# Gate steps of a tile pair spread between the weight units of the next pair, and a fourth quarter-product pair in the first layer

## The chip, the cores and the metric

One NeuronCore of one Trainium2 chip runs the whole program. The metric is the device time of one execution in microseconds, from the runs' own timer. The profiled execution also has a span, from its first instruction to its last.

## The reference, cut to what matters

Four transformer-like layers on one sequence of 512 tokens of 1024 channels, in float32. The first two layers (one with a causal convolution mixer, one with attention) each end in a feed-forward block, and this block is what the change touches:

```python
def conv_gated_ffn(x, w_up, w_gate, conv_w, conv_b, w_down):
    u = x @ w_up                                        # 1024 -> 2816
    g = causal_dwconv(x @ w_gate, conv_w, conv_b)       # three taps per channel
    return (jax.nn.silu(g) * u) @ w_down                # 2816 -> 1024
```

2816 channels are 22 tiles of 128. The last two layers (a gated linear attention beside a latent attention) and the convolution mixer are not touched.

## The kernel before, in words

**Split numbers.** Every weight is fetched as float32 and split into a high part (rounded to fp32r, tile wh) and a low remainder (wl); activations are split in the same way (XH and XL, HH and HL). A 128x128 block of weights then takes three matmuls: high by high, high by the activations' low part, low by high (function block, L618 records them). Activations lie transposed: channels on partitions, the 512 tokens along the free axis.

**The weight stream.** Weights come in units of 8 blocks (NU), in an order written out by hand (weight_order, and ffn_order at L45 for the feed-forward). SyncE fetches unit u to one of 3 raw buffers (L546, raw), once VectorE has made the remainder of unit u - 3. ScalarE rounds it to one of 4 slots (round_to, L1445), which waits until TensorE has used the unit that held the slot before. VectorE makes the remainder (rest_to, L2165). Both engines do this where their own program says so: feed_group(matrix, ks, cols) stands for the blocks that TensorE is then working on, and where one of these blocks is the first of a unit, the engine prepares the unit three further on (AHEAD). All engines run their programs strictly in order, so a step that waits holds up everything written after it.

**Tiles and pairs.** For the tiles f of the feed-forward TensorE makes up(f) and gate(f) over all 512 tokens: 8 blocks x 3 matmuls of 512 columns for each. The first PAIRS[layer] pairs of tiles (f = 2p and 2p + 1; 3 pairs in layer 0, 7 in layer 1, L23) are made by quarter products instead: tokens, input channels and tiles are halved, and seven products of 4 blocks x 3 matmuls of 256 columns replace eight. For a pair and each of the two matrices these are, in TensorE's order:

- A (up) and D (gate), first_products: 8 blocks, 24 matmuls
- C (up) and F (gate), summed_products: 16 blocks of summed weights (matrices tu and tg), 48 matmuls
- E (up of tile 2p + 1) and B (gate of tile 2p + 1, which comes in the next pair), last_product: 4 blocks, 12 matmuls

The order in time is A(p), B(p-1), C(p), D(p), E(p), F(p): 168 matmuls, 56 blocks, 7 units. The results are put together outside TensorE: ScalarE evacuates a bank twice for each matrix (first_out, second_out), VectorE adds five times (first_combined, three_combined, last_combined). The up results stand in sqr[0] and sqr[1], the gate results in gb[0] and gb[1] (acc_s and acc_q). E(p) waits for the second of the sums of three_combined(0, p), C(p)'s last product for first_combined(0, p), B(p-1) for the second sum of three_combined(1, p-1).

**The gate steps.** For each tile (gated, L1547 on ScalarE and L2340 on VectorE): ScalarE's bias step, VectorE's two taps, ScalarE's silu, VectorE's product with up, ScalarE's high part of the product (HH), VectorE's low part (HL). In a pair both engines write these as one piece for each tile: gated(f-2) stands between A(p)'s and C(p)'s units, gated(f-1) right behind B(p-1)'s, each engine waiting for the other at every step, and only then comes the preparation of the units for C(p) and, on ScalarE, the evacuation second_out(0, p).

**The summed weights.** They are made in device memory by GpSimd's DMAs (weight_sums, L3166) in four parts (SUMMED, L25: layer, first and last column group, the unit count at which the part begins, and the count between its steps). Each part is a chain of eight DMAs, alternately a copy and an adding DMA; each waits for the one before it to land. A fetch of a tu or tg piece waits on SyncE until its part is complete (raw, s.tw). Pairs 0 and 1 of layer 0 are part 0, pair 2 is part 1; parts 2 and 3 are layer 1's. A step of part 0 moves 1024 KB, one of part 1 512 KB.

## Time and profile before

| what | value |
|---|---|
| median of 3 runs | 1791.28 us (1789.99 to 1794.4) |
| profiled execution, its own time | 1790.65 us |
| its span | 1788.9 us |
| mean granted clock of TensorE | 0.987 of 2.4 GHz |
| TensorE matmuls, busy | 1742.5 us, 97% |
| VectorE, busy | 1150.7 us |
| ScalarE, busy | 896.7 us |

The profiled execution's time is its span and 1.75 us around it. Busy shares are means over stages with different limits; the stretches of the two feed-forward stages with quarter products are 251 to 330 us and 955 to 1130 us. In the rows a matmul whose moving operand is 256 columns wide is "128x256", and matmuls overlap, so the distance between starts tells the rate, not the duration.

### The profile page before, as it was taken

How to read it: one execution, taken by the hardware profiler on the slowest of the kernel's cores; microseconds unless marked ns; L12 is line 12 of the kernel's file. 1: busy time of each engine (PE TensorE's matmuls, PEld its weight loads, DVE VectorE, ACT ScalarE, POOL GpSimd, SP SyncE). 2: the span in 40 equal slices, each digit the busy share in tenths (PEclk: the TensorE clock that was granted, in tenths of full speed). 3: DMA queues.
4: the chain of work that ended last, by engine and by line, in shares of the span. 5: the costliest groups of instructions: out<-in, count | busy, mean ns of one | idle time of the engine just before them, and what ended most of it. 6: DMA issues, size and time to landing. Idle time of an engine off the chain costs nothing.

```text
span 1788.9 us, 24379 instructions
## 1 busy us (share of the span) xinstructions
PE 1742.5 (97%) x9933; PEld 1449.4 (81%) x9933; DVE 1150.7 (64%) x1812; ACT 896.7 (50%) x1408; POOL 40.2 (2%) x53
## 2 busy tenths in 40 slices
PE   9999998999999999999999888999999999999999
PEld 7877998888888887777788887888898876778766
DVE  6778886644433565887786666643368867657674
ACT  6889755433332355666564444432246454533542
POOL 0000100000000000000200000000000000000000
PEclk9999999999999999999999988999999999999999
DMA  5374265755446643311234353223322222132211
GB/s 212 129 219 112 82 198 155 246 166 165 130 151 190 189 130 118 95 48 60 71 115 145 118 162 128 99 95 107 103 85 92 94 60 71 63 102 85 69 60 47
DMA packets 59663, 213.22 MB, mean 119 GB/s; under 512 B 7072, under 2 KB 7328, under 8 KB 56608
## 3 DMA queue, kind: packets, MB, share of 16 engines
q1 hardware_dynamic: 56096, 169.73, 28.5%
q0 software_dynamic: 3456, 41.95, 8.9%
q8 instruction: 78, 1.28, 0.3%
q14 instruction: 33, 0.27, 0.0%
HBM read 207.45 MB, written 44.04 MB: 141 GB/s over the span
## 4 chain that ended last, share of the span: by engine, by line
PE 79%; DVE 11%; ACT 7%; issue 2%; DMA 1%; SPq 0%; ACTq 0%; DVEq 0%
PE bank L618 79%; DVE wl L2161 3%; ACT tmp L1437 2%; DVE tmp L2152 2%; ACT wh L1437 2%; DVE tmp L2149 1%; DMA wraw<-in_wstream 1%; DVE HL L2161 1%; DVE sqr L2152 1%; ACT taps L1437 1%; DVE XL L2161 1%; PE bank L1382 0%; DMA wraw<-tw 0%; ACT HH L1437 0%; DVE sbl L2161 0%
## 5 line engine op out<-in xcount | busy, mean ns | idle before, releaser
L2161 DVE TENSOR_TENSOR wl<-wraw,wh 128x1024 fp32r<-128x1024 f32 (+1 forms) x294 | 355.3, 1219 | 274.2 <-ACT wh L1437 273.5
L618 PE MATMUL bank<-XH,wh 128*128 128x512 f32 (+1 forms) x1424 | 526.9, 370 | 3.0 <-DVE wl L2161 1.0
L618 PE MATMUL bank<-XL,wh 128*128 128x512 f32 (+1 forms) x1424 | 517.0, 363 | 0.0
L618 PE MATMUL bank<-XH,wl 128*128 128x512 f32 (+1 forms) x1424 | 516.9, 363 | 0.0
L1437 ACT ACTIVATE wh<-wraw 128x1024 fp32r<-128x1024 f32 (+1 forms) x294 | 306.5, 1052 | 318.4 <-PE bank L618 265.8
L618 PEld LDWEIGHTS bank<-XH,wh 128*128 128x128 f32 x1424 | 268.7, 189 | 55.9 <-issue 9.4
L618 PEld LDWEIGHTS bank<-XH,wl 128*128 128x128 f32 x1424 | 268.7, 189 | 42.8
L618 PEld LDWEIGHTS bank<-XL,wh 128*128 128x128 f32 x1424 | 269.0, 189 | 39.8 <-issue 0.7
L618 PE MATMUL bank<-HL,wh 128*128 128x256 f32 (+1 forms) x740 | 223.4, 345 | 34.9 <-DVE sqr L2152 34.9
L618 PE MATMUL bank<-HH,wh 128*128 128x256 f32 (+1 forms) x740 | 223.2, 344 | 0.0
L618 PE MATMUL bank<-HH,wl 128*128 128x512 f32 (+1 forms) x580 | 202.9, 350 | 0.0
L618 PEld LDWEIGHTS bank<-HL,wh 128*128 128x128 f32 x740 | 137.1, 203 | 50.4 <-DVE sqr L2152 36.5
L618 PEld LDWEIGHTS bank<-HH,wh 128*128 128x128 f32 x740 | 135.6, 201 | 14.3 <-DVE Y L2152 0.6
L618 PEld LDWEIGHTS bank<-HH,wl 128*128 128x128 f32 x580 | 113.7, 196 | 13.1
L1437 ACT ACTIVATE tmp<-tmp 128x512 f32<-128x512 f32 (+2 forms) x131 | 72.4, 596 | 91.3 <-DVE tmp L2149 90.9
L2149 DVE SCALAR_TENSOR_TENSOR tmp<-bank,prm,tmp 128x511 f32<-128x511 f32 (+1 forms) x48 | 35.9, 749 | 80.1 <-ACT tmp L1437 79.2
L1437 ACT ACTIVATE tmp<-bank 128x512 f32<-128x512 f32 (+4 forms) x129 | 70.5, 567 | 14.7 <-PE bank L618 12.4
L1437 ACT ACTIVATE tmp<-bank,prm 128x512 f32<-128x512 f32 (+1 forms) x44 | 30.5, 696 | 92.3 <-PE bank L618 92.2
L2152 DVE TENSOR_TENSOR X<-X,bank 128x512 f32<-128x512 f32 (+1 forms) x58 | 38.5, 665 | 39.7 <-PE bank L618 39.7
L618 PE MATMUL bank<-XH,HL 128*128 128x256 f32 x256 | 57.4, 287 | 0.3 <-DVE XL L2161 0.2
L618 PE MATMUL bank<-wh,XH 128*128 128x512 f32 x128 | 50.7, 396 | 0.1
L2161 DVE TENSOR_TENSOR HL<-tmp,HH 128x512 fp32r<-128x512 f32 x44 | 30.5, 692 | 30.7 <-ACT HH L1437 30.7
(375 smaller groups left out, 2438.3 us busy)
## 6 DMA issues: line engine op xcount, KB each, us to landing
wraw<-in_wstream SPq DMA_DIRECT2D x256, 512.0 KB, 3.6
wraw<-tw SPq DMA_DIRECT2D x80, 256.0 KB, 3.2
tw<-in_w POOLq DMA_DIRECT2D x6, 1536.0 KB, 12.6
tw<-in_w POOLq DMA_DIRECT2D x4, 2048.0 KB, 15.5
wraw<-in_wstream SPq DMA_DIRECT2D x22, 256.0 KB, 2.9
tw<-in_w POOLq DMA_DIRECT2D x4, 1024.0 KB, 10.6
tw<-in_w POOLq DMA_DIRECT2D x6, 512.0 KB, 7.9
tw<-tw POOLq DMA_DIRECT2D x2, 1536.0 KB, 7.3
```

Source lines behind the costliest of these rows:

```text
L618: return pe.e.matmul(o, l, r, start=start, stop=stop, skip_group_check=True)
L1437: return act.e.activation(o, i, f, **kw)
L2149: return dve.e.scalar_tensor_tensor(out=o, in0=i0, scalar=sc, in1=i1, op0=op0, op1=op1)
L2152: return dve.e.tensor_tensor(o, i0, i1, op)
L2161: return dve.e.tensor_tensor(o, x, h.bitcast(F32), ALU.subtract)
```

## The change

- PAIRS goes from (3, 7) to (4, 7): tiles 6 and 7 of layer 0 are made by quarter products. Part 1 of the summed weights therefore covers column groups 4 to 8 instead of 4 to 6, at the same starting count and with the same eight steps, each now 1024 KB.
- The first pair of each layer has four empty blocks in place of B, so that in layer 0 each pair begins with a unit. The stream grows from 307 to 311 units; from layer 0's down projection to the end of layer 1 blocks lie half a unit further on than before.
- gated is cut into bias, silu and high on ScalarE and taps, product and low on VectorE, for each tile. The six steps of each of the two tiles of pair p - 1 are placed one by one between the preparations of pair p's units.
- VectorE's three_combined(1, p-1) and ScalarE's second_out(1, p-1) are written at the head of the next pair instead of at the end of their own. The numbering of the sums (SUMS) follows.
- The up results rotate over three buffers (sqr[0], sqr[1] and the new third), since the products of pair p - 1 are now made after part of pair p has been evacuated; first_out and second_out of up wait for the product that last read their buffer.
- TensorE's, SyncE's and GpSimd's programs are unchanged.

```diff
-PAIRS = (3, 7)
-
-SUMMED = [(0, 0, 4, 16, 1), (0, 4, 6, 38, 1), (1, 0, 6, 60, 4), (1, 6, 14, 100, 5)]
+PAIRS = (4, 7)
+
+SUMMED = [(0, 0, 4, 16, 1), (0, 4, 8, 38, 1), (1, 0, 6, 60, 4), (1, 6, 14, 100, 5)]
...
         out += [(up, k, f) for k in range(KD)]
-        if p:
-            out += [(gate, k, f - 1) for k in range(4, KD)]
+        out += [(gate, k, f - 1) for k in range(4, KD)] if p else [None] * 4
         out += [(tu, k, p) for k in range(16)] + [(gate, k, f) for k in range(KD)]
         out += [(up, k, f + 1) for k in range(4, KD)] + [(tg, k, p) for k in range(16)]
...
-    return [(p, 0, 1)] + [(p - 1, 1, 5)] * (p > 0) + [(p, 0, 2), (p, 0, 3), (p, 0, 4), (p, 1, 1), (p, 0, 5), (p, 1, 2), (p, 1, 3), (p, 1, 4)]
-
-
-SUMS = [[x for p in range(n) for x in sums_of_pair(p)] + [(n - 1, 1, 5)] for n in PAIRS]
+    before = [(p - 1, 1, j) for j in (2, 3, 4)] if p else []
+    return before + [(p, 0, 1)] + [(p - 1, 1, 5)] * (p > 0) + [(p, 0, 2), (p, 0, 3), (p, 0, 4), (p, 1, 1), (p, 0, 5)]
+
+
+SUMS = [[x for p in range(n) for x in sums_of_pair(p)] + [(n - 1, 1, j) for j in range(2, 6)] for n in PAIRS]
...
+    m.PP, m.HH, m.HL, m.pts, m.SF, m.third = [], [], [], [], [], []
...
+            m.third.append(sb(ph, f"third{layer}", [128, S]))
...
     m.gb = [m.acc_s, m.acc_q]
+    m.ub = [[[(m.sqr + [t])[(2 * p + j) % 3] for j in range(2)] for p in range(FT // 2)] for t in m.third]
...
-        def gated(f, g):
-
-            n = FT * layer + f
-            u, v = tmp[2 * f % 4], tmp[(2 * f + 1) % 4]
+        def bias(f, g):
+
             act.wait_ge(s.pg_x, 8 * layer + 8)
             if f >= 2:
-                act.wait_ge(s.f_h, n - 1)
-            fn(u[:, :], g[:, :], ACT.Identity, scale=P(f"fcw{layer}", 3 * f + 2), bias=P(f"fcb{layer}", f)).then_inc(s.f_u, 1)
-            act.wait_ge(s.f_conv, n + 1)
+                act.wait_ge(s.f_h, FT * layer + f - 1)
+            fn(tmp[2 * f % 4][:, :], g[:, :], ACT.Identity, scale=P(f"fcw{layer}", 3 * f + 2), bias=P(f"fcb{layer}", f)).then_inc(s.f_u, 1)
+
+        def silu(f):
+
+            u = tmp[2 * f % 4]
+            act.wait_ge(s.f_conv, FT * layer + f + 1)
             fn(u[:, :], u[:, :], ACT.Silu).then_inc(s.f_silu, 1)
-            act.wait_ge(s.f_h, n + 1)
-            fn(HH[:, f, :], v[:, :], ACT.Copy).then_inc(s.f_hi, 1)
-
-        def pair_gated(p, odd):
+
+        def high(f):
+
+            act.wait_ge(s.f_h, FT * layer + f + 1)
+            fn(HH[:, f, :], tmp[(2 * f + 1) % 4][:, :], ACT.Copy).then_inc(s.f_hi, 1)
+
+        def pair_bias(p, odd):
             act.wait_ge(s.u_c, combined(layer, p, 1, 4 + odd))
-            gated(2 * p + odd, m.gb[odd])
+            bias(2 * p + odd, m.gb[odd])
...
         def first_out(g, mat, p):
+            if g == 0 and p >= 2:
+                act.wait_ge(s.f_h, FT * layer + 2 * p - 2)
             act.wait_ge(s.stream, w.done(mat, KD - 1, 2 * p))
-            fn((sqr, m.gb)[g][0][:, 0:256], bank[3 * g][:, 0:256], ACT.Copy).then_inc(s.u_e, 1)
+            fn((m.ub[layer][p], m.gb)[g][0][:, 0:256], bank[3 * g][:, 0:256], ACT.Copy).then_inc(s.u_e, 1)
 
         def second_out(g, mat, p):
+            if g == 0 and p:
+                act.wait_ge(s.f_h, FT * layer + 2 * p - 1)
             act.wait_ge(s.stream, w.done(mat, 15, p))
-            fn((sqr, m.gb)[g][1][:, 0:256], bank[3 * g][:, 0:256], ACT.Copy).then_inc(s.u_e, 1)
+            fn((m.ub[layer][p], m.gb)[g][1][:, 0:256], bank[3 * g][:, 0:256], ACT.Copy).then_inc(s.u_e, 1)
 
         for p in range(PAIRS[layer]):
             f = 2 * p
+            if p:
+                second_out(1, tg, p - 1)
             feed_group(up, range(KD), [f])
             if p:
-                pair_gated(p - 1, 0)
+                pair_bias(p - 1, 0)
             first_out(0, up, p)
             if p:
                 feed_group(gate, range(4, KD), [f - 1])
-                pair_gated(p - 1, 1)
-            feed_group(tu, range(16), [p])
+            feed_group(tu, range(4), [p])
+            if p:
+                pair_bias(p - 1, 1)
+            feed_group(tu, range(4, 12), [p])
+            if p:
+                silu(f - 2)
+            feed_group(tu, range(12, 16), [p])
+            feed_group(gate, range(4), [f])
+            if p:
+                silu(f - 1)
             second_out(0, tu, p)
-            feed_group(gate, range(KD), [f])
+            feed_group(gate, range(4, KD), [f])
+            feed_group(up, range(4, KD), [f + 1])
+            if p:
+                high(f - 2)
             first_out(1, gate, p)
-            feed_group(up, range(4, KD), [f + 1])
-            feed_group(tg, range(16), [p])
-            second_out(1, tg, p)
+            feed_group(tg, range(8), [p])
+            if p:
+                high(f - 1)
+            feed_group(tg, range(8, 16), [p])
+        last = PAIRS[layer] - 1
+        second_out(1, tg, last)
         for f in range(2 * PAIRS[layer], FT):
             feed_group(up, range(KD), [f])
             if f == 2 * PAIRS[layer]:
-                pair_gated(PAIRS[layer] - 1, 0)
+                pair_bias(last, 0)
                 feed_group(gate, range(4, KD), [f - 1])
-                pair_gated(PAIRS[layer] - 1, 1)
+                pair_bias(last, 1)
+                silu(f - 2)
+                silu(f - 1)
+                high(f - 2)
+                high(f - 1)
             feed_group(gate, range(KD), [f])
             act.wait_ge(s.stream, w.done(gate, KD - 1, f))
-            gated(f, bank[gate_bank(f)])
+            bias(f, bank[gate_bank(f)])
+            silu(f)
+            high(f)
...
-        def gated(f, bu, bg):
-
-            n = FT * layer + f
-            u, v = tmp[2 * f % 4], tmp[(2 * f + 1) % 4]
-            dve.wait_ge(s.f_u, n + 1)
+        def taps(f, bg):
+
+            u = tmp[2 * f % 4]
+            dve.wait_ge(s.f_u, FT * layer + f + 1)
             t = dve.mark(stt(u[:, 1:S], bg[:, 0:S - 1], P(f"fcw{layer}", 3 * f + 1), u[:, 1:S], ALU.mult, ALU.add))
             dve.wait_ge(dve.own, t)
             stt(u[:, 2:S], bg[:, 0:S - 2], P(f"fcw{layer}", 3 * f), u[:, 2:S], ALU.mult, ALU.add).then_inc(s.f_conv, 1)
-            dve.wait_ge(s.f_silu, n + 1)
-            tt(v[:, :], u[:, :], bu[:, :], ALU.mult).then_inc(s.f_h, 1)
-            dve.wait_ge(s.f_hi, n + 1)
-            less(HL[:, f, :], v[:, :], HH[:, f, :]).then_inc(s.f_lo, 1)
+
+        def product(f, bu):
+
+            dve.wait_ge(s.f_silu, FT * layer + f + 1)
+            tt(tmp[(2 * f + 1) % 4][:, :], tmp[2 * f % 4][:, :], bu[:, :], ALU.mult).then_inc(s.f_h, 1)
+
+        def low(f):
+
+            dve.wait_ge(s.f_hi, FT * layer + f + 1)
+            less(HL[:, f, :], tmp[(2 * f + 1) % 4][:, :], HH[:, f, :]).then_inc(s.f_lo, 1)
...
-            b, (o, _) = bank[3 * g:3 * g + 3], (sqr, m.gb)[g]
...
+            b, (o, q) = bank[3 * g:3 * g + 3], (m.ub[layer][p], m.gb)[g]
...
-            q = (sqr, m.gb)[g][1]
...
         for p in range(PAIRS[layer]):
             f = 2 * p
+            if p:
+                three_combined(1, p - 1)
             feed_group(up, range(KD), [f])
-            if p:
-                gated(f - 2, sqr[0], m.gb[0])
             first_combined(0, p)
             if p:
+                taps(f - 2, m.gb[0])
+                last_combined(1, p - 1)
+                dve.wait_ge(s.u_c, combined(layer, p - 1, 1, 5))
                 feed_group(gate, range(4, KD), [f - 1])
-                last_combined(1, p - 1)
-                gated(f - 1, sqr[1], m.gb[1])
-            feed_group(tu, range(16), [p])
+            feed_group(tu, range(12), [p])
+            if p:
+                product(f - 2, m.ub[layer][p - 1][0])
+                taps(f - 1, m.gb[1])
             three_combined(0, p)
-            feed_group(gate, range(KD), [f])
+            feed_group(tu, range(12, 16), [p])
+            feed_group(gate, range(4), [f])
+            if p:
+                product(f - 1, m.ub[layer][p - 1][1])
+            feed_group(gate, range(4, KD), [f])
+            feed_group(up, range(4, KD), [f + 1])
             first_combined(1, p)
-            feed_group(up, range(4, KD), [f + 1])
+            if p:
+                low(f - 2)
             last_combined(0, p)
             dve.wait_ge(s.u_c, combined(layer, p, 0, 5))
-            feed_group(tg, range(16), [p])
-            three_combined(1, p)
+            feed_group(tg, range(8), [p])
+            if p:
+                low(f - 1)
+            feed_group(tg, range(8, 16), [p])
+        last = PAIRS[layer] - 1
+        three_combined(1, last)
         for f in range(2 * PAIRS[layer], FT):
             feed_group(up, range(KD), [f])
             if f == 2 * PAIRS[layer]:
-                gated(f - 2, sqr[0], m.gb[0])
+                taps(f - 2, m.gb[0])
+                last_combined(1, last)
+                dve.wait_ge(s.u_c, combined(layer, last, 1, 5))
                 feed_group(gate, range(4, KD), [f - 1])
-                last_combined(1, PAIRS[layer] - 1)
-                gated(f - 1, sqr[1], m.gb[1])
+                taps(f - 1, m.gb[1])
+                product(f - 2, m.ub[layer][last][0])
+                product(f - 1, m.ub[layer][last][1])
+                low(f - 2)
+                low(f - 1)
             feed_group(gate, range(KD), [f])
-            gated(f, bank[(2 + 2 * f) % 6], bank[gate_bank(f)])
+            taps(f, bank[gate_bank(f)])
+            product(f, bank[(2 + 2 * f) % 6])
+            low(f)
```

## Rows read from the trace of the kernel before

**Rows 1.** The page: busy shares, and the chain that ended last by engine
```profile
PE 1742.5 (97%) x9933; PEld 1449.4 (81%) x9933; DVE 1150.7 (64%) x1812; ACT 896.7 (50%) x1408; POOL 40.2 (2%) x53
PE 79%; DVE 11%; ACT 7%; issue 2%; DMA 1%; SPq 0%; ACTq 0%; DVEq 0%
```

**Rows 2.** Waits of TensorE, first layer (244:315), then second (959:1130): total, times, longest
```profile
PE bank L618 <- DVE sqr L2152: 8.7, 2, 4.4
...
PE bank L618 <- DVE sqr L2152: 26.1, 6, 4.4
```

**Rows 3.** Table by stretch: us, busy PE, PEld, DVE, ACT, POOL, clock, DMA, GB/s
```profile
984.95:1012.30 27.35, 23.00 (x170) 22.75 (x169) 17.57 (x26) 12.32 (x17) 0.00 (x0) 0.88 0.41 132
988.00:998.00 10.00, 10.00 (x84) 9.92 (x83) 6.63 (x10) 3.69 (x7) 0.00 (x0) 1.00 0.23 87
1002.50:1008.00 5.50, 5.48 (x25) 5.48 (x26) 3.32 (x5) 1.06 (x1) 0.00 (x0) 0.50 0.87 266
1123.30:1323.00 199.70, 199.70 (x921) 167.03 (x920) 85.89 (x99) 62.98 (x75) 0.00 (x0) 1.00 0.29 98
...
270.16:296.89 26.73, 22.32 (x170) 21.71 (x169) 18.54 (x27) 14.59 (x19) 0.78 (x1) 0.94 0.62 179
296.89:323.24 26.35, 21.98 (x171) 21.74 (x170) 16.99 (x25) 11.73 (x17) 0.53 (x1) 0.94 0.53 193
```

**Rows 4.** TensorE in order of time: start, us, what, [idle before and its releaser]
```profile
1002.52 0.79 PE L618 MATMUL bank<-HL,wh 128*128 128x256 f32 x2 [4.35 <-DVE sqr L2152]
```

**Rows 5.** ScalarE in order of time: round, evacuation, bias step, silu, table load
```profile
983.77 1.06 ACT L1437 ACTIVATE wh<-wraw 128x1024 fp32r<-128x1024 f32 x1 [2.00 <-PE bank L618]
985.15 0.38 ACT L1437 ACTIVATE acc_q<-bank 128x256 f32<-128x256 f32 x1 [0.32 <-PE bank L618]
987.62 0.80 ACT L1437 ACTIVATE tmp<-acc_s,prm 128x512 f32<-128x512 f32 x1
996.32 0.63 ACT L1437 ACTIVATE tmp<-tmp 128x512 f32<-128x512 f32 x1 [1.60 <-DVE tmp L2149]
...
961.03 1.28 ACT L1437 ACT_TABLE_LOAD   x1
```

**Rows 6.** VectorE in order of time: two taps, product, two remainders, two of three sums
```profile
994.75 1.54 DVE L2149 SCALAR_TENSOR_TENSOR tmp<-acc_q,prm,tmp 128x511 f32<-128x511 f32 x2 [0.89 <-ACT tmp L1437]
996.98 0.69 DVE L2152 TENSOR_TENSOR tmp<-tmp,sqr 128x512 f32<-128x512 f32 x1 [0.70 <-ACT tmp L1437]
999.32 2.36 DVE L2161 TENSOR_TENSOR wl<-wraw,wh 128x1024 fp32r<-128x1024 f32 x2 [0.26 <-ACT wh L1437]
1001.60 0.41 DVE L2152 TENSOR_TENSOR sqr<-sqr,bank 128x256 f32<-128x256 f32 x1
1002.04 0.42 DVE L2152 TENSOR_TENSOR sqr<-bank,sqr 128x256 f32<-128x256 f32 x1
```

**Rows 7.** TensorE and the table by stretch, where a shorter gap stood (convolution stage)
```profile
131.44 0.50 PE L618 MATMUL bank<-cinh,HH 32*128 32x512 f32 x4 [0.99 <-DVE cinl L2161]
...
131.00:140.00 9.00, 8.09 (x96) 6.29 (x96) 8.34 (x13) 8.71 (x15) 0.00 (x0) 1.00 0.78 162
```

**Rows 8.** GpSimd's DMAs: three steps of part 0, then part 1's first
```profile
93.71 0.83 POOL L3164 DMA_DIRECT2D tw<-in_w  x1 [13.37 <-DVE wl L2161]
105.95 0.52 POOL L3160 DMA_DIRECT2D tw<-tw  x1 [11.41 <-DMA tw<-in_w]
111.90 0.82 POOL L3164 DMA_DIRECT2D tw<-in_w  x1 [5.43 <-DMA tw<-tw]
...
225.65 0.54 POOL L3160 DMA_DIRECT2D tw<-in_w  x1 [20.12 <-DVE wl L2161]
```

**Rows 9.** DMA issues (size, median us to landing), and ScalarE awaiting a unit beside one
```profile
wraw<-in_wstream SPq DMA_DIRECT2D x256, 512.0 KB, 3.6
tw<-in_w POOLq DMA_DIRECT2D x4, 1024.0 KB, 10.6
...
321.36 1.06 ACT L1437 ACTIVATE wh<-wraw 128x1024 fp32r<-128x1024 f32 x1 [4.40 <-DMA wraw<-in_wstream]
```

More of the change, by code:

```diff
@@ L430, in place @@
         m.cinl = ring(ph, "cinl", 2, [128, PAD + S], FR)
-    m.PP, m.HH, m.HL, m.pts, m.SF = [], [], [], [], []
+    m.PP, m.HH, m.HL, m.pts, m.SF, m.third = [], [], [], [], [], []
     for layer in range(2):
@@ L2347, in gated @@
             stt(u[:, 2:S], bg[:, 0:S - 2], P(f"fcw{layer}", 3 * f), u[:, 2:S], ALU.mult, ALU.add).then_inc(s.f_conv, 1)
-            dve.wait_ge(s.f_silu, n + 1)
-            tt(v[:, :], u[:, :], bu[:, :], ALU.mult).then_inc(s.f_h, 1)
-            dve.wait_ge(s.f_hi, n + 1)
-            less(HL[:, f, :], v[:, :], HH[:, f, :]).then_inc(s.f_lo, 1)
+        def product(f, bu):
[4 more added lines that the diff above has]
+            less(HL[:, f, :], tmp[(2 * f + 1) % 4][:, :], HH[:, f, :]).then_inc(s.f_lo, 1)
         def first_combined(g, p):
-            b, (o, _) = bank[3 * g:3 * g + 3], (sqr, m.gb)[g]
+            b, (o, _) = bank[3 * g:3 * g + 3], (m.ub[layer][p], m.gb)[g]
             dve.wait_ge(s.u_e, 4 * (pairs_before(layer) + p) + 2 * g + 1)
@@ L2359, in three_combined @@
         def three_combined(g, p):
-            b, (o, q) = bank[3 * g:3 * g + 3], (sqr, m.gb)[g]
+            b, (o, q) = bank[3 * g:3 * g + 3], (m.ub[layer][p], m.gb)[g]
             dve.wait_ge(s.u_e, 4 * (pairs_before(layer) + p) + 2 * g + 2)
@@ L2367, in last_combined @@
         def last_combined(g, p):
-            q = (sqr, m.gb)[g][1]
+            q = (m.ub[layer][p], m.gb)[g][1]
             dve.wait_ge(s.stream, w.done(("up", "gate")[g] + str(layer), KD - 1, 2 * p + 1))
```

## The prediction

> **What bounds the kernel now.** The page comes first: TensorE is busy for 97% of the span and carries 79% of the chain that ended last; VectorE and ScalarE carry 18% between them [rows 1]. So the time can fall only where that chain leaves TensorE. The waits say where: TensorE waits for VectorE's sums into sqr six times in the second feed-forward and twice in the first, some 4.4 us each, once in every pair but the first [rows 2]. The table by stretch gives the price. From A(p) to A(p+1) of the second layer, 984.95 to 1012.30, it is 27.35 us [rows 3]. The pair's matmuls are 168, and 84 of their kind take 10.00 us (0.12 us each), so 20.16 us would do: 7.19 us are lost. About 4.5 us are the wait [rows 4]; behind it the clock stands at 0.50 for 5.5 us, the lower level of 1.2 GHz, and 25 matmuls take what 46 would [rows 3]; that is the rest. In layer 0 the two pairs take 26.73 and 26.35 us, an excess of 6.57 and 6.19. The wait is E(p)'s for three_combined(0, p), which both engines reach only after the whole ping-pong of gated(f-1) and two remainders; the rows of VectorE show just this order [rows 6].
>
> A plain tile pair for comparison: 96 matmuls of 512 columns at 199.70 us for 921, 0.217 us each, 20.8 us [rows 3].
>
> **The change, layer 1.** No matmul is added or removed, and each pair's work on VectorE (17.57 us) and ScalarE (12.32 us) stays [rows 3]; it fits under 20.16 us if the order does. I walk one pair, t = 0 at A(p); segments end at A 2.88, B 4.32, C 10.08, D 12.96, E 14.40, F 20.16. Blocks lie so that a unit begins at the fifth block of A, at C's first and ninth, D's first, E's first, F's fifth and thirteenth. Durations are round 1.06, evacuation 0.38, bias 0.80, silu and high 0.63, two taps 1.54, product and low 0.69, remainder 1.2, the second sum ending 0.86 after the first begins [rows 5, 6]; ScalarE starts 0.20 after TensorE has passed a boundary (985.15 against 984.95).
> - ScalarE: second_out(1) from 0.2, round from 1.7 (its slot is free at 1.44), bias(f-2) to 3.5, first_out(0) to 3.7, round from 4.5 to 5.6. VectorE: three sums to 2.2, remainder to 4.0, first_combined, taps(f-2) to 5.8, last_combined to 6.2, remainder to 7.3; ScalarE's bias(f-1) 6.2 to 7.0.
> - The next round may start only when TensorE has passed C's eighth block, 7.20: 7.4 to 8.5. Behind it silu(f-2) to 9.0 and VectorE's remainder to 9.7, product(f-2) to 10.3, taps(f-1) to 11.8. ScalarE's next round waits for C's end and runs 10.3 to 11.4; silu(f-1) 11.9 to 12.5; second_out(0) to 12.8; VectorE's second sum to 13.7. TensorE wants E at 12.96 and gets it at 13.74: it waits 0.78 us.
> - After that: product(f-1) 15.8, first_combined(1) 17.2 (wanted at 19.5), two lows, last_combined and two remainders, the last at 22, which is 1.0 in the next pair, in time for B at 2.88. A raw unit is fetched when the remainder three units back is done and lands 3.6 us later [rows 9], each time before ScalarE's turn.
>
> So a pair takes 20.16 + 0.78 = 20.94 us. A gap of that size keeps the clock: one of 0.99 us in the convolution stage stands in a stretch with the clock at 1.00 [rows 7]. Saved: 27.35 - 20.94 = 6.4 us, six times, 38.4 us. In pair 1 the table load, 1.28 us [rows 5], stands before the first silu and now delays second_out by some 0.7: 37.7 us are left. The third buffer costs nothing: second_out(0) waits for product(f-2), done at 10.3, 2 us before. Were that cover gone, the wait would add to the 0.78. The last pair's steps lie beside a plain tile (up(14) and B, 6.6 us, then gate 5.2) and stay hidden.
>
> The Trainium skill, page "TensorE: Matmul & The Clock Gate", section "A second HAM failure mode: psum-queue depth-cycling", speaks against this: frequent short idles of TensorE between groups of matmuls can make the clock fall again and again, though none is long. By the row of the 0.99 us gap the sum is as above; by that rule it would be a rival's, below.
>
> **Layer 0.** The walk is kinder here, since units begin with the pairs: the rounds ahead of silu(f-2) and silu(f-1) may start at 5.96 and 8.84, taps(f-1) ends at 10.8, the second sum at 12.7, before 12.96. Pair 1 with its table load waits about 0.5. Left alone, the two excesses of 12.76 us would fall to 1, and the fourth pair would be 20.16 against 20.8.
>
> But part 1 of the summed weights has twice the bytes. GpSimd starts it at 225.65 as before. A step of 1024 KB takes 12.24 us as an adding DMA (93.71 to 105.95) and 5.95 as a copy (105.95 to 111.90) [rows 8]; with the median of 10.6 to landing plus 0.8 issue, 11.4 for an add [rows 9], eight steps are 4 x 11.4 + 4 x 5.95 = 69.4 us, and the part is ready at 295. Pair 2 needs it. Pair 1 starts at 270.16 as before and pair 2's A ends, at the new pace, at 270.16 + 20.16 + 0.5 + 2.88 = 293.7. SyncE comes to the unit with B and C's first blocks at about 279 and stands there till 295; behind it on SyncE are the fetches of the next two units, and ScalarE, in order, stands at that unit's round, with high(f-1), second_out(1) and the biases queued behind it. After 295: landing 3, round 1.1, remainder 1.2, the next remainder, then three_combined(1, 1): its second sum comes at about 303.8, and only then may B(2) run. TensorE idles 10 us, and pays the half clock once more (2.5 us). The rest of pair 2 is 144 matmuls, 17.3 us: A(3) at 303.8 + 2.5 + 17.3 = 323.6. Part 2's 1536 KB steps now fall on pair 3, where before ScalarE awaited a unit for 4.4 us beside such a step [rows 9]: I take 21.5 us for pair 3. up(8) starts at 345.1, B(3) follows, gate(8) at 345.1 + 5.2 + 1.44 = 351.7. Before: A(2) ended its pair at 323.24 [rows 3]; then 24 + 72 matmuls at 0.217, B's 1.44 and up(8)'s 24: 350.7. Layer 0 costs 1 us instead of gaining 12.
>
> The Trainium skill, page "DMA: Bandwidth & Descriptors", section "Anatomy of one DMA", gives GpSimd's DMAs 2.0 us plus bytes by 436 GB/s, 4.4 us for 1 MB. The sum by that would have part 1 ready at 261 and layer 0's 12 us gained. Its figure is for a fetch from device memory to on-chip memory; the rows of this same chain, 5.95 to 12.24, decide.
>
> **Small ones.** Four more units give VectorE 4.9 us and ScalarE 4.2 us of work, all in stages where TensorE is the later (plain tiles: VectorE 86 of 200 us [rows 3]); without that cover they would cost 5. Parts 2 and 3 and the norm's sums behind them on GpSimd move with their unit counts. The half unit by which layer 1's blocks shift alters which waits fall where in its attention and norms; no row prices it. It could gain or lose some waits of the size of the 0.99 us gap; I take 0 and keep 2 us to either side.
>
> **Sum.** 1790.65 - 37.7 + 1 = 1754.0 us against the profiled execution's own time, which lies 0.6 below the median; 1754.
>
> **Rivals.**
> - Part 1 is ready early enough, or pair 1 is slow enough, that SyncE's stop costs nothing: layer 0 gains about 11. For it: the steps of this size are rowed in another stage, beside the convolution's traffic. Against: the chain would have to be done by 283, with steps of 7.2 us on average. This is also where the Trainium skill's fit, above, would lead. 1790.65 - 37.7 - 11 = 1742. Chance 0.12.
> - The steps still collide: VectorE, 17.6 of 20.9 us filled, falls behind, and each pair waits 2 to 3 us more (one extra round or remainder ahead of second_out(0), 1.1 to 2.3). Seven such pairs, 15 us: 1769. Chance 0.12.
> - The clock falls after the short waits too, by the rule named above: 2.5 us in seven pairs, 17 us: 1771. Against: the 0.99 us gap. Chance 0.05.
> - Slower: part 1's chain starves. From about 250 SyncE wants 11.2 us of all DMA engines for each pair (0.41 of 27.35) [rows 3], now in 20.9 us, beside steps twice as large, and everything waits on SyncE behind tu(2). It turns the sign only if the part is ready 38 us later, at 333, with steps of 13.5 us on average where the dearest row is 12.24. At 340: 1798. Chance 0.02.
> - The change doesn't do what it says: the sums of three_combined(1, p-1), now a pair later in VectorE's order, hold B(p-1) for as long as E was held, and the time stays: 1790. Against: walk, 2.0 against 2.88. Chance 0.02.
>
> The forecast has 0.67. The range holds the first two rivals' near ends and the shift of 2 us: 1741 to 1769. A difference under 0.3% (5 us) can't be told from none. Faster 0.95: all but the last two; same 0.02; slower 0.03.
>
> **What would show it.** Right: in the second layer TensorE's waits for sqr fall from 4.4 to under 1 us, A to A near 21 us, clock near 1.00; in the first, one wait of about 10 us before 304, behind a fetch of tw, and GpSimd's eighth step of part 1 near 284. Wrong: that wait missing (1742), a clock of 0.9 with short gaps, or A to A of 23 us with ScalarE's second evacuation late.

## The result, and the profile after

The changed kernel takes 1773.37 us in the median of four runs (1772.04 to 1775.91), the kernel before 1790.94 beside it: the ratio is 0.990, with a 95% interval of 0.9883 to 0.9917. That is 17.6 us faster. The forecast was 1754.0 with a range of 1741 to 1769: the sign was right, the size was not, and the time lies above the range. The profiled execution took 1773.67 us, its span is 1771.9 us.

The page after, busy shares, and the chain that ended last by engine (they answer to [rows 1]):

```profile
PE 1731.8 (98%) x10005; PEld 1442.0 (81%) x10005; DVE 1157.3 (65%) x1826; ACT 901.1 (51%) x1416; POOL 40.2 (2%) x53
...
PE 78%; DVE 10%; ACT 7%; DMA 3%; issue 2%; SPq 0%; ACTq 0%; DVEq 0%
```

TensorE is still the chain. DMA's share of it went from 1% to 3%.

To find where 17.0 us of span went, I mark the same points of the program in both traces and subtract. A pair's matmuls are the first of 256 columns after the stage before, so A(0) is easy to find.

| stretch | before, us | after, us | difference |
|---|---|---|---|
| start to A(0) of layer 0 | 251.44 | 249.46 | -2.0 |
| pair 0 of layer 0, A(0) to A(1) | 18.72 | 27.11 | +8.4 |
| pair 1 | 26.73 | 24.69 | -2.0 |
| pair 2 | 26.35 | 20.16 | -6.2 |
| tiles 6 and 7, up(8) and B, to gate(8) | 28.68 | 33.95 | +5.3 |
| gate(8) to A(1) of layer 1 (attention within) | 605.6 | 622.1 | +16.5 |
| A(1) to up(14) of layer 1 | 164.02 | 127.00 | -37.0 |
| the rest | 667.3 | 667.4 | +0.1 |

The first line lies ahead of every instruction that the change touches; it is drift between two executions (over the traces of this case A(0) begins anywhere from 248.98 to 253.22 us). Three things matter: the line from A(1) to up(14), which is the forecast's gain almost to the microsecond; layer 0, which costs 5.4 us instead of 1; and the stage between, which was taken at nothing and costs 16.5.

Before, gate(8) begins at 351.92 and not at 350.7, as the prediction had it. Between two matmuls of 512 columns lie 0.226 us and not 0.217, as this row of the kernel before shows, which holds no others (729 in 165.00 us):

```profile
1135.00:1300.00 165.00, 165.00 (x729) 136.67 (x729) 70.76 (x78) 54.03 (x63) 0.00 (x0) 1.00 0.30 99
```

**Layer 1.** The table by stretch, the six periods and then one (columns as in [rows 3]):

```profile
977.46:1104.46 127.00, 122.50 (x1010) 121.28 (x1009) 103.42 (x151) 75.20 (x103) 0.00 (x0) 1.00 0.55 174
1023.21:1044.24 21.03, 20.41 (x170) 20.21 (x169) 17.22 (x26) 12.33 (x18) 0.00 (x0) 1.00 0.55 180
```

TensorE in order of time, the waits of pairs 1 and 2 of layer 1 (they answer to [rows 4]):

```profile
992.00 0.51 PE L620 MATMUL bank<-HL,wh 128*128 128x256 f32 x2 [1.42 <-DVE sqr L2185]
1013.03 0.51 PE L620 MATMUL bank<-HL,wh 128*128 128x256 f32 x2 [0.62 <-DVE third L2185]
```

Compare with [rows 3, 4]: 27.35 us at clock 0.88 became 21.03 at clock 1.00. The wait is the same one, E(p)'s for a sum into the up buffer, and it is 0.62 us instead of 4.35 (it costs 0.87: 21.03 against the 20.16 of a pair without a wait). Pair 1 has 0.8 us more, the table load.

**The attention stage.** TensorE's waits there, total, times and longest:

```profile
PE bank L620 <- DVE wl L2194: 10.0, 1, 10.0
PE bank L620 <- DVE OL L2194: 1.7, 1, 1.7
PE bank L620 <- DVE X L2182: 1.0, 1, 1.0
PE bank L620 <- DVE OH L2182: 0.8, 1, 0.8
```

Before, the largest wait between 600 and 900 us was 0.3 us. One wait of 10.0 us for a remainder (wl) is new. VectorE in order of time at that place, TensorE there, and the table by stretch just behind it:

```profile
644.52 0.42 DVE L2194 TENSOR_TENSOR XL<-X,XH 128x256 fp32r<-128x256 f32 x1 [0.71 <-ACT XH L1439]
644.86 3.49 DVE L2194 TENSOR_TENSOR wl<-wraw,wh 128x1024 fp32r<-128x1024 f32 x3
```

```profile
646.23 0.55 PE L620 MATMUL bank<-XH,wh 128*128 128x256 f32 x1 [9.96 <-DVE wl L2194]
```

```profile
646.00:649.00 3.00, 2.77 (x13) 2.81 (x14) 2.35 (x3) 0.38 (x1) 0.87 (x1) 0.50 0.58 169
```

VectorE is busy with the norm's chain (X to tmp to XL, tile by tile) and comes to its three remainders only after the last XL; TensorE starts again 1.4 us after they begin, when the first of them is there. Behind the gap the clock is 0.50. What the gap costs with its half clock, the table by stretch tells, from the first matmul of 256 columns at the norm to the last, before and after: 12.3 us more, 9.96 of them the wait and some 2.4 the half clock.

```profile
603.52:645.86 42.34, 41.98 (x338) 41.17 (x336) 34.05 (x73) 26.75 (x52) 0.52 (x1) 1.00 0.43 143
606.99:661.67 54.68, 44.36 (x337) 43.38 (x336) 32.93 (x72) 26.73 (x52) 0.87 (x1) 0.91 0.48 141
```

Here is why a block's place in its unit matters. While the norm runs, TensorE works through the q and k blocks of channel tiles 0 to 7 as each tile is normalised. Their first unit comes in the ordinary order and the next three are prepared ahead, in spare buffers. Before, these blocks began with unit 117, and four units held all of them. Now they begin in the middle of unit 120, the last tile's blocks lie in unit 124, a fifth one, and no spare holds it: its remainder comes in the ordinary order, after the last XL. The trace of before shows the same three remainders right behind the last XL, with no gap on TensorE: it did not need them yet.

```profile
641.05 0.42 DVE L2161 TENSOR_TENSOR XL<-X,XH 128x256 fp32r<-128x256 f32 x1 [0.71 <-ACT XH L1437]
641.39 3.49 DVE L2161 TENSOR_TENSOR wl<-wraw,wh 128x1024 fp32r<-128x1024 f32 x3
```

**Layer 0.** TensorE's waits in order of time, then ScalarE's before them, then GpSimd's steps of part 1:

```profile
258.05 0.50 PE L620 MATMUL bank<-HH,wh 128*128 128x256 f32 x2 [1.24 <-DVE sqr L2185]
266.94 0.80 PE L620 MATMUL bank<-HL,wh 128*128 128x256 f32 x2 [4.32 <-DVE sqr L2185]
292.46 0.58 PE L620 MATMUL bank<-HL,wh 128*128 128x256 f32 x2 [2.78 <-DVE sqr L2185]
339.03 0.80 PE L620 MATMUL bank<-HL,wh 128*128 128x256 f32 x2 [4.49 <-DVE sqr L2185]
```

```profile
264.64 1.06 ACT L1439 ACTIVATE wh<-wraw 128x1024 fp32r<-128x1024 f32 x1 [5.71 <-DMA wraw<-tw]
265.61 0.37 ACT L1439 ACTIVATE sqr<-bank 128x256 f32<-128x256 f32 x1
...
289.65 1.06 ACT L1439 ACTIVATE wh<-wraw 128x1024 fp32r<-128x1024 f32 x1 [3.64 <-DMA wraw<-tw]
...
332.76 1.06 ACT L1439 ACTIVATE wh<-wraw 128x1024 fp32r<-128x1024 f32 x1 [4.79 <-DMA wraw<-tw]
```

```profile
245.20 0.81 POOL L3223 DMA_DIRECT2D tw<-in_w  x1 [5.07 <-DVE wl L2194]
255.50 0.52 POOL L3219 DMA_DIRECT2D tw<-tw  x1 [9.48 <-DMA tw<-in_w]
261.26 0.81 POOL L3223 DMA_DIRECT2D tw<-in_w  x1 [5.24 <-DMA tw<-tw]
272.77 0.52 POOL L3219 DMA_DIRECT2D tw<-in_w  x1 [10.71 <-DMA tw<-in_w]
278.39 0.82 POOL L3223 DMA_DIRECT2D tw<-in_w  x1 [5.10 <-DMA tw<-in_w]
...
320.00 0.85 POOL L3223 DMA_DIRECT2D tw<-in_w  x1 [10.96 <-DVE wl L2194]
```

Read the three together. (The first wait, of 1.24 us, is C(0)'s last product's for first_combined(0, 0); the others are E's.) At 264.64 ScalarE rounds a unit of summed weights for which it waited 5.71 us, and the evacuation that E(0) needs stands right behind it; TensorE goes on at 266.94. The fetch was under way from 258.06 to 264.62, first beside the copy of 255.50 and then beside the adding DMA of 1024 KB that began at 261.26. The fetches of the units of 289.65 and 332.76 were issued with an adding DMA already under way, that of 278.39 and part 2's 1536 KB of 320.00. Issued at 279.91 and 322.44, they took 9.7 and 10.3 us to landing:

```profile
wraw<-tw SPq DMA_DIRECT2D x1, 256.0 KB, 9.7
wraw<-tw SPq DMA_DIRECT2D x1, 256.0 KB, 10.3
```

ScalarE's waits for such units, 244 to 345 us, were 11.2 us in four; after:

```profile
ACT wh L1439 <- DMA wraw<-tw: 29.8, 8, 7.3
```

SyncE, which was to stand for 16 us, waits for part 1 for 3.3 us only:

```profile
SPq L561 <- DMA tw<-in_w: 3.3, 1, 3.3
```

The table by stretch for pairs 1, 2 and 3 of layer 0. Pair 2 is free of waits and takes exactly its 20.16 us; pair 3, forecast at 21.5, takes 27.05:

```profile
276.57:301.26 24.69, 21.91 (x171) 21.71 (x169) 17.40 (x25) 13.39 (x18) 0.82 (x1) 0.93 0.76 211
301.26:321.42 20.16, 20.16 (x171) 20.16 (x169) 16.69 (x25) 12.22 (x17) 1.37 (x2) 1.00 0.73 243
321.42:348.47 27.05, 22.56 (x171) 22.36 (x170) 18.02 (x26) 12.10 (x17) 0.53 (x2) 0.87 0.88 269
```

### The profile page after: what moved, and what is told of

The parts are those of the page before. It is cut to its first block, busy times and chain, and to the rows that moved or that the text cites. A ratio compares the mean times of both kernels' runs of the same rounds, so it can differ in the third digit from the quotient of the medians.

```text
span 1771.9 us, 24583 instructions
## 1 busy us (share of the span) xinstructions
PE 1731.8 (98%) x10005; PEld 1442.0 (81%) x10005; DVE 1157.3 (65%) x1826; ACT 901.1 (51%) x1416; POOL 40.2 (2%) x53
## 4 chain that ended last, share of the span: by engine, by line
PE 78%; DVE 10%; ACT 7%; DMA 3%; issue 2%; SPq 0%; ACTq 0%; DVEq 0%
PE bank L620 77%; DVE tmp L2185 3%; DVE wl L2194 2%; ACT tmp L1439 2%; ACT wh L1439 2%; DMA wraw<-tw 1%; DMA wraw<-in_wstream 1%; DVE XL L2194 1%; DVE tmp L2182 1%; DVE sqr L2185 1%; ACT taps L1439 1%; DVE HL L2194 1%; PE bank L1384 0%; ACT X L1439 0%; DVE HH L2194 0%
## 5 line engine op out<-in xcount | busy, mean ns | idle before, releaser
L2194 DVE TENSOR_TENSOR wl<-wraw,wh 128x1024 fp32r<-128x1024 f32 (+1 forms) x298 | 361.2, 1220 | 304.6 <-ACT wh L1439 303.3
L1439 ACT ACTIVATE wh<-wraw 128x1024 fp32r<-128x1024 f32 (+1 forms) x298 | 312.2, 1053 | 370.6 <-PE bank L620 316.1
L620 PE MATMUL bank<-HL,wl 128*128 128x256 f32 x176 | 51.4, 292 | 0.0
## 6 DMA issues: line engine op xcount, KB each, us to landing
tw<-in_w POOLq DMA_DIRECT2D x6, 1536.0 KB, 11.5
tw<-in_w POOLq DMA_DIRECT2D x8, 1024.0 KB, 10.3
tw<-in_w POOLq DMA_DIRECT2D x4, 2048.0 KB, 15.1
```

Source lines behind the costliest of these rows:

```text
L620: return pe.e.matmul(o, l, r, start=start, stop=stop, skip_group_check=True)
L1439: return act.e.activation(o, i, f, **kw)
L2194: return dve.e.tensor_tensor(o, x, h.bitcast(F32), ALU.subtract)
```

## The experiments

Two questions. For the 16.5 us of the attention stage: is it the place of the blocks in their units (the half unit by which they moved), or something else that the change brought there, such as later transfers? For layer 0: is it the transfers (twice the bytes in part 1, and part 2 beside the fourth pair), or the order on ScalarE, which puts second_out(0) behind rounds that wait for them? Every edit is against the changed kernel, but for e2.

### e1 and e2: four empty blocks ahead of the q and k blocks

```diff
         if layer == 1:
+            o += [None] * 4
             o += [(mat, k, c) for k in range(KD) for mat in ("wq", "wk") for c in range(2)]
```

e1 puts them into the changed kernel, where they undo the half unit; e2 puts them into the kernel before, where they make it.

> The kernel after, with four empty blocks put into the weight stream before layer 1's query and key blocks, so that these begin with a unit again, as before the change. Theory A (the half unit puts the last channel tile's blocks of the norm's head outside the units prepared ahead, and TensorE waits 9.96 us for them and then runs at half clock): the wait is gone, -12 to -15 us; layer 1's pairs then begin with a unit too, so the 0.62 us in each goes as well, -4 us: 1755 to 1760 us. Theory B (the four units more in the stream, or the transfers, cause the wait, not the position): 1770 to 1774 us and the wait stays.

> The kernel before, with nothing but four empty blocks before layer 1's query and key blocks (so they begin in mid-unit, as in the kernel after). Theory A: a wait of about 10 us in the norm before them and its half clock, 1801 to 1806 us. Theory B: 1789 to 1793 us, no such wait.

e1 took 1773.37 us, ratio 0.9892 (0.9868 to 0.9916): no faster than the change. e2 took 1825.09 us, ratio 1.0189 (1.0170 to 1.0208): 34 us slower than the kernel before. TensorE's waits between 600 and 1420 us, e1 and then e2:

```profile
PE bank L621 <- DVE wl L2195: 11.8, 2, 11.4
```

```profile
PE bank L619 <- DVE sqr L2153: 29.2, 7, 4.8
PE bank L619 <- DVE wl L2162: 22.0, 4, 11.4
```

e2 is the clean proof: nothing but the place of the blocks differs from the kernel before (and one unit more in the stream), and TensorE has the wait of 9.9 us for wl at 645.68. From the norm's first matmul of 256 columns to layer 1's A(0) it takes 15.1 us more than the kernel before (350.45 against 335.32); the change takes 15.7 more. e2 was 19 us slower than the upper end of its expectation, which forgot that a shift made ahead of layer 1 lasts to the layer's end: a second wait, of 11.4 us, stands at 1372.79, before the input blocks of the next layer, where the same head of a norm comes again. From there to the end of the run e2 takes 17.4 us more than the kernel before. That explains e1 as well. The wait at 646 is gone there, but its four blocks move everything behind them, and the 11.4 us appear at 1322.08. In the changed kernel layer 1's feed-forward brings its own four empty blocks and so mends the second norm; e1 mended the first and broke the second. My expectation for e1 did not foresee that.

### e5: the empty blocks behind each layer's feed-forward

```diff
         o += grouped(f"down{layer}", FT, list(range(8)), 1)
+        o += [None] * 4
```

> The kernel after, with four empty blocks behind each layer's down projection: layer 1's query and key blocks, its feed-forward and layer 2's input blocks all begin with a unit, as before the change. If the half unit costs wherever a norm's head follows: neither the 10 us wait before the attention nor the 11.4 us wait that the first experiment showed before layer 2; layer 1's pairs begin with a unit and their waits of 0.6 us are gone: 1773.4 - 12.6 - 4.4 = 1756, 1754 to 1759 us.

1758.64 us, ratio 0.9809 (0.9794 to 0.9824): 14.7 us less than the change. No wait of 10 us is left in either place. The pairs of layer 1 begin with a unit now, and their waits are gone too (one of 0.4 us). In TensorE's waits of 600 to 1420 us four of over 1 us are left, two at each norm:

```profile
PE bank L621 <- DVE acc_q L2186: 3.5, 2, 1.7
PE bank L621 <- DVE XL L2183: 1.5, 1, 1.5
PE bank L621 <- DVE XL L2195: 1.5, 1, 1.5
```

### e3: three pairs in layer 0 again

```diff
-PAIRS = (4, 7)
+PAIRS = (3, 7)
-SUMMED = [(0, 0, 4, 16, 1), (0, 4, 8, 38, 1), (1, 0, 6, 60, 4), (1, 6, 14, 100, 5)]
+SUMMED = [(0, 0, 4, 16, 1), (0, 4, 6, 38, 1), (1, 0, 6, 60, 4), (1, 6, 14, 100, 5)]
```

> The kernel after, with three pairs in layer 0 again and the second part of the summed weights at its old size; the order of steps, the empty blocks and the half unit as in the kernel after. Theory C (the fourth pair costs by its doubled transfers: units of summed weights land late behind them, and the evacuation stands behind such a unit on ScalarE): the waits of E in pairs 0 and 1 of layer 0 shrink below 1 us together and the fourth pair's 4.5 us wait is gone: 1758 to 1764 us. Theory D (layer 0's waits come from the new order alone, transfers being only what ends last): pairs 0 and 1 wait as in the kernel after (4.3 and 2.8 us), only the fourth pair's wait goes: 1766 to 1770 us.

1761.29 us, ratio 0.9833 (0.9814 to 0.9852), 12 us less than the change. TensorE waits 0.57, 1.30 and 2.89 us in layer 0 instead of 12.8 in all. The time is theory C's and E(0)'s wait all but goes (0.57 us), but E(1)'s stays (2.89 us, 2.78 with the change), which theory C did not have. Ahead of it stand 3.09 us at 275.20, in which ScalarE waits for a fetch beside a step of the old 512 KB, and pair 1's table load of 1.28 us; what share each has, no run tells. ScalarE's waits for summed weights fell to a third:

```profile
ACT wh L1439 <- DMA wraw<-tw: 10.6, 4, 7.4
```

### e4: second_out(0) ahead of the last rounds

```diff
+            second_out(0, tu, p)
             feed_group(tu, range(12, 16), [p])
             feed_group(gate, range(4), [f])
             if p:
                 silu(f - 1)
-            second_out(0, tu, p)
```

> The kernel after, with ScalarE's second_out(0, tu, p) moved ahead of the preparation of units during tu 12 to 15 and of silu(f-1). If the position behind a late unit's round is what holds E(p): the wait of 4.3 us in pair 0 of layer 0 goes (-7 us with its half clock), that of 2.8 in pair 1 falls below 1, the seven of 0.6 us in layer 1 fall to 0 to 0.2; the fourth pair's stays, its late unit being ahead of silu(f-2): 1758 to 1762 us. If TensorE would wait for the late unit itself anyway: the waits only change their releaser to a remainder of a unit, and the time falls by the 4 us of layer 1 alone, 1769 us.

1762.32 us, ratio 0.9838 (0.9820 to 0.9856), 11 us less than the change. ScalarE still waits 27.8 us for summed weights (29.8 with the change), but what stands behind them is no longer what TensorE needs next. The wait of E(0) is gone; left are 1.45 us at 258, 3.35 at 276.8 (B(0), for acc_q; under 1 was expected in pair 1) and 4.02 at 333. The pairs of layer 1 wait for 0.36 us once, though they still begin in mid-unit. So both theories hold a part: the late transfers are the cause, and the order decides whether TensorE feels them.

### e6 to e10: both together, and the place of the parts

All five have e5's blocks and e4's order. e6 also has three pairs; e7 begins part 2 at unit count 75 instead of 60, behind the fourth pair; e8 is e7 with part 1 at 30 instead of 38; e9 has neither, and so tells what part 2's place alone is worth; e10 is e8 with three pairs.

```diff
-SUMMED = [(0, 0, 4, 16, 1), (0, 4, 8, 38, 1), (1, 0, 6, 60, 4), (1, 6, 14, 100, 5)]
+SUMMED = [(0, 0, 4, 16, 1), (0, 4, 8, 30, 1), (1, 0, 6, 75, 4), (1, 6, 14, 100, 5)]
```

> As the experiment before it, with second_out(0) early and layer 0's three pairs and small transfers again: all parts that were seen to help. Effects adding up: 1773.4 - 17 (units) - 12 (three pairs) and little more for second_out, whose layer 1 gain the units take already: 1742 to 1748 us. If layer 0's three pairs and second_out act on the same waits only partly, towards 1742; if the 1.7 and 1.3 us waits at the norm that came with the units stay, towards 1748.

> Four pairs, units and second_out early as above; part 2 of the summed weights (layer 1's first three pairs, 1536 KB a step) begins at unit 75 instead of 60, behind layer 0's pairs. If layer 0's fourth pair waits because its summed unit lands late beside that part's adding DMA: the 4 us wait near 335 and its half clock go, about 6 us less than with part 2 in place (1762.3 - 12.6 for that, so 1744 us); if it waits for other reasons: 1749 to 1751 us with the wait in place.

> As the experiment before it, and part 1 begins at unit 30 instead of 38, so that its eight steps of 1024 KB start some 20 us sooner and half of them are done when pair 0 starts. If the wait in pair 1 (3.4 us at 277 with second_out early) comes from those steps: it is gone or under 1 us, 5 us less than the run before; if the steps only move their trouble into the norm and the gate of the embedding ahead, the same time or more, with new waits between 205 and 250.

> Four pairs, units whole, second_out(0) early, both parts of the summed weights where the change has them. It stands between the runs already made: if part 2's adding DMA beside the fourth pair is worth what its wait and half clock were (4 + 2.5 us), 1752 to 1754 us (1746.1 with part 2 late, 1758.6 without the early evacuation); if the later part 2 gained by something else, 1746 to 1748 us and no wait near 330.

> The same with three pairs in layer 0 and small steps of part 1, part 1 beginning at unit 30 and part 2 at 75. If the fourth pair costs only by its transfers, it costs nothing once these are out of the way, and three pairs are no faster than four with the same starts (1741.2): 1740 to 1743 us. If the fourth pair costs something of itself (3.5 more units to fetch and split, its own waits): 1737 to 1739 us.

| kernel | pairs | part 1, 2 begin at | us | ratio (95%) | TensorE's waits in layer 0, us |
|---|---|---|---|---|---|
| e9 | 4 | 38, 60 | 1751.66 | 0.9762 (0.9746 to 0.9777) | 1.93, 1.81, 1.22, 5.06 |
| e7 | 4 | 38, 75 | 1746.11 | 0.9741 (0.9727 to 0.9756) | 0.49, 1.08, 4.00 |
| e8 | 4 | 30, 75 | 1741.16 | 0.9711 (0.9696 to 0.9725) | 2.75 |
| e6 | 3 | 38, 60 | 1743.66 | 0.9738 (0.9707 to 0.9768) | 1.68, 0.90 |
| e10 | 3 | 30, 75 | 1743.00 | 0.9709 (0.9690 to 0.9729) | none |

The kernels were compared with the kernel before in two sets of runs (1792.2 us for e6 to e8, 1793.5 for e9 and e10), so the ratios are what stands side by side. The 5.06 us of the fourth pair in e9 is part 2's, as e9's waits of 320 to 345 us show (ScalarE for a unit, and TensorE behind it):

```profile
ACT wh L1440 <- DMA wraw<-tw: 6.0, 1, 6.0
PE bank L621 <- DVE sqr L2186: 5.1, 1, 5.1
```

With part 2 moved out of the way, in e7, it is gone, and with part 1 begun eight units sooner, in e8, the one of 4.00 us too. e7 lies 2 us above its 1744, e9 0.3 us below its 1752; the others are where they were expected. Then three or four pairs make no difference that can be told (0.9709 and 0.9711). The fourth pair itself was to bring 0.6 us (1.6 by the rate of plain tiles as the trace has it), and it brings nothing that these runs can resolve; what it cost in the change was its transfers. The wait that e8 has left is C(0)'s for first_combined(0, 0). Shortly before, ScalarE had stood 10.56 us for a unit of summed weights, and VectorE's steps run without a break from that unit to the sum; no run takes this wait away by itself, so its cause is argued and not shown.

```profile
250.68 1.06 ACT L1440 ACTIVATE wh<-wraw 128x1024 fp32r<-128x1024 f32 x1 [10.56 <-DMA wraw<-tw]
```

That e10 has none is in part chance: its A(0) began 3.5 us later (253.22 against 249.73), and its sum, at 260.27, was no earlier than e8's, at 259.36.

### e11 and e12: the empty blocks ahead of the down projection

What was still open were the 1.7 and 1.5 us at each norm in e5 to e10. The kernel before did not have them, and it began its down projection with a unit.

```diff
+        o += [None] * 4
         o += grouped(f"down{layer}", FT, list(range(8)), 1)
```

e11 is the change with this alone; e12 has e8's order and parts as well.

> Change kernel with four empty blocks ahead of each layer's down projection (e5_units had them behind it), so that the down projection too begins with a unit, as in the kernel before. Theory: the 1.73 and 1.47 us waits at each of the two norms of e5_units (6.4 us in all) come from a down projection that begins in the middle of a unit. They go, no wait of 10 us comes back, layer 0 keeps its waits of 0.8, 3.9, 3.2 and 5.3 us: 1758.6 - 6.4 = 1752 us (1750 to 1754). Rival: they come from the number of units or from the transfers, and stay wherever the empty blocks are: 1758 to 1760.

> The same padding with second_out(0) moved ahead of the last rounds, part 1's start at 30 and part 2's at 75, as in e8_units_early_parts (1741.2 us, ratio 0.9711). Theory: the norms' waits go here too and layer 0 keeps its one wait of 2.8 us: 1741.2 - 6.4 = 1735 us, ratio about 0.9675. Rival: the waits stay, 1741.

e11: 1754.02 us, ratio 0.9785 (0.9769 to 0.9802). e12: 1734.29 us, ratio 0.9675 (0.9661 to 0.9689). The waits at the norms are gone in both; these are all of e12's between 600 and 1420 us, and then its one in layer 0:

```profile
PE bank L621 <- DVE X L2183: 0.5, 2, 0.3
PE bank L621 <- DVE XL L2183: 0.3, 1, 0.3
PE bank L621 <- DVE OH L2183: 0.3, 1, 0.3
PE bank L621 <- DVE XL L2195: 0.3, 1, 0.3
```

```profile
PE bank L621 <- DVE sqr L2186: 3.0, 1, 3.0
```

e11 lies 2 us above the sum expected; its layer 0 waits for 15.6 us where e5's did for 13.2. Four kernels have the same program up to there, and their waits spread: 12.8 (the change), 13.2 (e5), 15.6 (e11) and 15.8 us (e1). e12 is the fastest kernel of this study: 57 us under the kernel before and 39 under the change.

## Why the prediction was wrong, point by point

- **What bounds the kernel, and layer 1's term: right.** Predicted 37.7 us, measured 37.0. A pair was walked at 20.94 us and takes 21.03; E waits 0.62 us where the walk had 0.78, and 1.42 in the pair with the table load where it had 1.5. Nothing else in the pair waits, so the rival in which the steps still collide is out. No run separates the spreading of the gate steps from the moved sums and evacuation (three_combined(1) and second_out(1)): the 37.0 us are what both bring together.
- **The clock: right.** Seven waits of 0.48 to 1.42 us, one in each pair, and the clock is 1.00 throughout, in pair 0 and in the 127 us of the other six. The Trainium skill, page "TensorE: Matmul & The Clock Gate", section "A second HAM failure mode: psum-queue depth-cycling", would have the clock fall through frequent short idles; with idles of this length, once in 21 us, this trace doesn't agree.
- **The step that failed: the half unit under "Small ones".** It was taken at 0 with 2 us to either side, "some waits of the size of the 0.99 us gap". It costs 16.5 us between gate(8) and layer 1's A(1): 9.96 us for the remainder of a unit that the spares no longer hold, 2.4 us for the half clock behind it, 3.4 us for three waits that grew in the rest of the stage (0.84, 0.99 and 1.71 us, from 0.3 or less each), and 0.7 us in layer 1's pair 0, where E now waits for 0.48. (With whole units, in e5, pair 0 has no wait.) e2 shows the shift alone, in the kernel before. e11 took 19.4 us off the change by undoing it everywhere, 5.9 of them in layer 1's pairs (from their A(0) to up(14) 140.6 us instead of 146.5). The mistake was one of kind, not of arithmetic: I said that the shift alters "which waits fall where", and priced it by a small wait that stood in the trace, when what counts is whether a whole unit is asked for before a long chain on VectorE and made behind it. The trace of before had it: the three remainders stand right behind the last XL (641.39), so nothing that lies in their units can be used while the norm runs. Finding the first block of each unit around the norm would have shown it.
- **Layer 0: right cost in kind, wrong place and size.** Predicted one stop of 10 us at B(2), +1 in all; measured +5.4 and no such stop. Part 1 was faster than costed: its first seven steps took 54.8 us (223.64 to 278.39) where the sum had 58.0, it began 2 us sooner, and A(2) came at 301.26, not 290.8, since pairs 0 and 1 were late. So it was nearly ready when asked for (3.3 us on SyncE). That is the first rival's condition, all but met, and yet its 11 us did not come. What I left out is that the steps slow the fetches of pairs 0 and 1 that run beside them, and that the new order puts an evacuation behind such a fetch: E(0), which never waited before, waits 4.32 us (0.57 with the small steps of e3, none with the evacuation ahead in e4). I costed the transfers as a thing to be complete by a time, and not as a load on the transfers beside them, although the row of the 4.40 us [rows 9] showed just that for part 2, and was used for pair 3 alone (1.3 us; it was 6.9).
- **A plain pair's price was read wrong.** The 0.217 us come from 921 matmuls in 1123.3 to 1323.0, a stretch that also holds matmuls of 256 columns (B's, and the norm's from 1314.81 on). At 0.226 us a plain pair takes 21.8 us, so the fourth pair is worth 1.6 us and not 0.6, and before, gate(8) begins at 351.9: the sum for layer 0 would have been 0 instead of +1. Nothing else hangs on it. The chances of the rivals add up to 0.96 for faster and 0.02 for slower, where the line behind them has 0.95 and 0.03.
- **The Trainium skill's fit** (page "DMA: Bandwidth & Descriptors", section "Anatomy of one DMA") makes an estimate of 4.4 us for 1 MB. The trace doesn't agree for these DMAs within device memory: the copies of part 1 come 5.6 to 6.4 us after one another, the adding ones 9.6 to 11.5.
- **The sum.** With the measured terms, 1790.65 - 2.0 + 5.4 + 16.5 - 37.0 + 0.1 = 1773.65; the profiled execution took 1773.67. The 2.0 are drift, which happened to go the forecast's way. The range was too narrow because the one term with no row was bounded by what was near it, not by what it could do.

## What to carry to other kernels

When a change adds blocks to a stream of weights in fixed units, write down for each stage behind it which block opens a unit, above all where an engine is tied up in a long chain and units were prepared ahead for it; half a unit cost 16 of the 37 us gained here, and four empty blocks in the right place gave them back. On an engine that runs in order, put what the bounding engine needs next ahead of anything that waits for a transfer. Cost a background transfer twice: when it is complete, and what it does to the fetches beside it.

## What the runs showed of the hardware that was not expected

- Waits of up to 1.42 us left TensorE's clock at 1.00 (977.46 to 1104.46), while those of 2.78 us and more have stretches under it around them (0.93 and 0.87 in pairs 1 and 3 of layer 0, 0.50 right behind the 9.96 us). The length alone does not decide: behind 1.93 us in e9 (at 259.65) the clock was 0.50 from 259.8 to 263.1, behind 2.23 us in e1 (at 258.58) it stayed 1.00.
- GpSimd's adding DMA of 1024 KB takes nearly twice the copy's time, from issue to the next issue: 9.6, 10.3 and 11.5 us against 5.6 to 6.4. A unit of summed weights fetched beside one keeps ScalarE waiting for up to 7.3 us. These fetches of 256 KB take 3.0 us to landing in the median of the whole run, 4.0 in the stretch from 244 to 345 us, and 9.7 and 10.3 us in the two shown above, issued while an adding DMA was under way:

```profile
wraw<-tw SPq DMA_DIRECT2D x88, 256.0 KB, 3.0
```

```profile
wraw<-tw SPq DMA_DIRECT2D x31, 256.0 KB, 4.0
```

- A wait of 10 us costs about 12.3: in the attention stage some 2.4 us more went on matmuls at clock 0.50 behind it, by the difference of the two stretches above.
